# First two expert weight chunks split inside the eighth linear attention tile, a fourth split buffer for the first expert, gather rows cleared in that tile

## What is computed

```python
h = h + concat(o_gla, o_diff) @ w_out
xn = rms_norm(h, norm2_g)
g_w, g_idx = top_k(softmax(xn @ wg + bg), 1)        # one of 4 groups
e_w, e_idx = top_k(softmax(chosen group's 8 logits), 2)
for each of the 32 experts e, over the tokens routed to it:
    out[token] += weight * ((silu(x @ w1[e]) * (x @ w3[e])) @ w2[e])
```

## Time and profile before

| what | value |
|---|---|
| three runs | 1260.25, 1263.06 and 1264.33 us, median 1263.06 us |
| profiled execution | 1262.13 us |
| its span, first to last instruction | 1260.3 us |
| PE busy | 1162.5 us, 92% |
| DVE busy | 890.6 us, 71% |
| ACT busy | 690.3 us, 55% |
| POOL busy | 252.4 us, 20% |
| mean granted TensorE clock | 0.962 of full |

### The profile page before, as it was taken

The page is one execution under the profiler, slowest core; times in us unless marked ns, Lnnn a source line. Parts: engine busy times, 40 slices in busy tenths (PEclk is TensorE's granted clock), DMA queues, the critical chain, the costliest instruction groups (busy, mean ns, idle before and its releaser), DMA issues. The chain is left out here.

```text
span 1260.3 us, 17095 instructions
## 1 busy us (share of the span) xinstructions
PE 1162.5 (92%) x5875; PEld 875.0 (69%) x5876; DVE 890.6 (71%) x1310; ACT 690.3 (55%) x913; POOL 252.4 (20%) x324
## 2 busy tenths in 40 slices
PE   5989999889988779999669999999999999999993
PEld 4868887567766468888546777777777777777772
DVE  4434324655566467887658999999999999999881
ACT  5424204343543353343237777777777777777771
POOL 2212103321110021222341221221122122112100
PEclk9999999999999789999779999999999999999997
DMA  8030210200200243433479999999999999999941
GB/s 309 37 98 1 100 67 1 76 25 27 92 26 17 76 144 109 149 130 144 184 287 378 372 386 371 372 390 379 370 379 388 373 370 395 381 365 379 388 113 26
DMA packets 67426, 273.34 MB, mean 217 GB/s; under 512 B 13156, under 2 KB 19880, under 8 KB 42664
## 3 DMA queue, kind: packets, MB, share of 16 engines
q1 hardware_dynamic: 56744, 245.32, 50.5%
q0 software_dynamic: 7168, 20.98, 7.3%
q10 hardware_dynamic: 3456, 6.29, 1.3%
HBM read 248.44 MB, written 28.32 MB: 220 GB/s over the span
## 5 line engine op out<-in xcount | busy, mean ns | idle before, releaser
L1851 DVE TENSOR_TENSOR main_w_low<-w_raw,main_w_high 128x2048 fp32r<-128x2048 f32 x192 | 438.9, 2287 | 55.7 <-ACT main_w_high L1847 55.7
L1847 ACT CAST main_w_high<-w_raw 128x2048 fp32r<-128x2048 f32 x192 | 365.9, 1908 | 80.4 <-PE main_score L1865 52.6
L1777 POOL DMA_INDIRECT main_xg<-xn_dram,main_token x32 | 76.2, 2381 | 381.3 <-DVE main_token L1757 376.6
L1863 PE MATMUL main_pt<-main_w_high,main_xT_high 128*96 128x512 f32 x256 | 104.3, 408 | 1.2 <-DVE main_xT_low L2007 1.2
L1863 PE MATMUL main_score<-main_w_high,main_hT_high 128*96 128x512 f32 x256 | 103.2, 403 | 1.2 <-DVE main_hT_low L2019 1.2
L1863 PE MATMUL main_po<-main_w_high,main_xT_high 128*96 128x512 f32 x256 | 101.4, 396 | 2.8 <-DVE main_w_low L1851 2.8
L1865 PE MATMUL main_pt<-main_w_high,main_xT_low 128*96 128x512 f32 x256 | 102.8, 402 | 0.0
L1864 PE MATMUL main_pt<-main_w_low,main_xT_high 128*96 128x512 f32 x256 | 102.1, 399 | 0.0
L1865 PE MATMUL main_po<-main_w_high,main_xT_low 128*96 128x512 f32 x256 | 101.7, 397 | 0.0
L1865 PE MATMUL main_score<-main_w_high,main_hT_low 128*96 128x512 f32 x256 | 101.2, 395 | 0.0
L1864 PE MATMUL main_po<-main_w_low,main_xT_high 128*96 128x512 f32 x256 | 101.0, 395 | 0.0
(11 more groups left out here) (301 smaller groups left out, 2346.0 us busy)
## 6 DMA issues: line engine op xcount, KB each, us to landing
w_raw<-in_moe_w SPq DMA_DIRECT2D x192, 1024.0 KB, 10.4
slot_raw<-in_w_in SPq DMA_DIRECT2D x12, 1024.0 KB, 7.3
main_x<-in_x SPq DMA_DIRECT2D x8, 512.0 KB, 11.1
slot_raw<-in_w_out SPq DMA_DIRECT2D x4, 1024.0 KB, 6.3
main_hx<-in_x SPq DMA_DIRECT2D x8, 512.0 KB, 3.9
out<-main_hx SPq DMA_DIRECT2D x8, 512.0 KB, 2.6
xn_dram<-main_xn SPq DMA_DIRECT2D x8, 512.0 KB, 2.8
gr_dram<-main_stage ACTq DMA_DIRECT2D x8, 256.0 KB, 2.0
```

The lines of the kernel that those rows point to most:

```text
L1777: nc.gpsimd.indirect_dma_start(xg[u][:], None, s["xn2_dram"], bass.IndirectOffsetOnAxis(token[u][:, 0:1], 0), bounds_check=bound["x"], oob ...
L1847: nc.scalar.copy(wh[slot(c, e)][:], raw[u][c // 2][:, c % 2, :]).then_inc(w_high, 1)
L1851: nc.vector.tensor_tensor(wl[slot(c, e)][:], raw[u][c // 2][:, c % 2, :], wh[slot(c, e)][:].bitcast(F32), ALU.subtract).then_inc(w_low, 1)
L1863: nc.tensor.matmul(out, x_hi, w_hi, start=start, stop=False)
```

## The change

Six edits. (1) ACT casts chunks 0 and 1 of expert 0 at the end of its tile n = 7. (2) DVE subtracts chunk 0 in its tile n = 7, between `position` and `h_norm`; chunk 1 stays behind `list_token` but now waits until POOL's counter stands at the second gather. (3) DVE no longer makes the carried state after the last tile, which nothing reads; what waited for it waits for `g_o_mm`, PE's last product of that tile. (4) A fourth pair, `w_high3` and `w_low3`, takes chunk 5 of expert 0, so that the casts of its chunks 4 and 5 wait for the residual adds of tile 7 instead of a freed pair, and stand ahead of `act_x`; the raw buffer of these two chunks moves from 152 to 68 KiB. The first casts of expert 1 may run one chunk further ahead, and two loads of expert 2 wait for `chunk_used` 4. (5) SP issues chunks 0 and 1 of expert 1 at the start of n = 8 and chunks 4 and 5 of expert 0 after the first residual add of tile 7. (6) POOL clears `xg0` and `xg1` inside its tile n = 7.

```diff
-RAW_PAIRS = ((200, 104, 152), (168, 120, 136))
+RAW_PAIRS = ((200, 104, 68), (168, 120, 136))
...
+    def first_high(act, c):
+
+        act.wait_ge(s["raw_in"][0][c], 16)
+        nc.scalar.copy(w_first[0][c][:], s["raw_pair"][0][0][:, c, :]).then_inc(w_split_high, 1)
+
+    def first_low(dve, c):
+
+        dve.wait_ge(w_split_high, c + 1)
+        dve.wait_ge(g_o_mm, T)
+        nc.vector.tensor_tensor(w_first[1][c][:], s["raw_pair"][0][0][:, c, :], w_first[0][c][:].bitcast(F32),
+                                ALU.subtract).then_inc(w_split_low, 1)
...
             elif n == T:
-                sp.wait_ge(state_ready, T + 1)
-                for e, c in ((0, 4), (0, 5), (1, 0), (1, 1)):
-                    load_chunk(sp, a, s, e, e, c)
+                sp.wait_ge(g_o_mm, T)
+                for c in (0, 1):
+                    load_chunk(sp, a, s, 1, 1, c)
+                sp.wait_ge(added, 2 * T - 1)
+                for c in (4, 5):
+                    load_chunk(sp, a, s, 0, 0, c)
...
                     store_hxT(n - 1, half)
+                if n == T - 1:
+                    for c in range(2):
+                        first_high(act, c)
...
             h_root(n - 1)
+            if n == T - 1:
+                pool.wait_ge(g_o_mm, T)
+                clear_rows(0)
             if n < T:
                 g_root(n)
                 if n >= 2:
                     weights_of(pool, n - 2)
+            if n == T - 1:
+                pool.wait_ge(g_normed, T)
+                clear_rows(1)
...
-                carry(n)
+                if n + 1 < T:
+                    carry(n)
                 if n >= 2:
                     position(n - 2)
+                if n == T - 1:
+                    first_low(dve, 0)
...
         if isinstance(e, int) and e == 0:
-            return {0: 1, 1: 2, 4: 0, 5: 2}[c]
+            return {0: 1, 1: 2, 4: 0, 5: 3}[c]
...
         if isinstance(e, int) and e == 0:
-            if c == 5:
-                act.wait_ge(chunk_used, 2)
+            if c == 4:
+                act.wait_ge(after["added"], 2 * T - 1)
+            elif c == 5:
+                act.wait_ge(after["added"], 2 * T)
         else:
-            act.wait_ge(chunk_used, n - 1 if isinstance(e, int) and (e, c) == (1, 1) else n - 2)
+            act.wait_ge(chunk_used, n - 3 if isinstance(e, int) and e == 1 and c < 3 else n - 2)
...
             for k in range(2):
                 list_row(dve, k)
                 pick(q, k + 2, k + 2, k)
+                if k == 0:
+                    low(dve, 0, 0, 5)
...
     def scalar(act):
-        for chunk in range(2):
+        for chunk in (4, 5):
             high(act, 0, 0, 0, chunk)
         act_x(act, 0, 0)
...
-        for chunk in range(2):
-            low(dve, 0, 0, chunk)
+        dve.wait_ge(after["pool_step"], front["own"]["gathers"] + 2)
+        front["first_low"](dve, 1)
         dve_x(dve, 0, 0)
```

## The result

| kernel | median of its runs | ratio to before, 95% interval |
|---|---|---|
| before | 1262.88 us (1260.25 to 1264.33, 4 runs) | |
| after | 1253.96 us (1253.29 to 1255.11, 4 runs) | 0.9929 (0.9915 to 0.9943) |

A forecast was written before the change was run, and what follows sets the result against it. PE was taken to set the pace from expert 1 on, so an earlier expert start ends the kernel earlier. +3.8 - 4.6 - 7.2 = -8.0 us gave a forecast of 1254.7 us, range 1252.0 to 1260.3.

The forecast's parts named there:

- Term 1, the delay of `turn`: Tile 8: DVE's subtraction waits for ACT's cast and delays what follows; 3.2 us reach the chain through PE's `turn`.
- Term 1, the clock: Tile 8's output product on PE: after a longer gap it runs longer at the low clock, taken as 0.6 us.
- Term 2: First gather of expert 0: starting ahead of DVE's subtraction, it runs as if alone; -4.6 us, bounds -2.0 and -4.6.
- Term 3: Start of the experts, first gate chunk to expert 1's down product: PE's waits shrink; -7.2 us, bounds -5.7 and -8.1.
- two named parts: Expert 0 into expert 1: hidden transposes 5.7 us earlier, and the gate chunk behind them back at full clock, 1.5 us.
- the lower end: Lower end of the range, 1252.0 us: includes up to 0.6 less where the clock rises earlier in gate chunk 0.
- The cover of ACT's new casts: Casts of chunks 4 and 5 ahead of `act_x`: done at 631, transposes at 636.3, a cover of 5 us.
- The edits costed at nothing: POOL's clears and ACT's casts in tile 8, expert 1's later first loads, SP's wait for `chunk_used` 4: no cost.
- The caught gather: Rival at the first gather: one subtraction still catches it, gain only -2.0, sum -5.4, 1257.3 us; chance 0.30.
- The eaten head start: Rival: clock and new gaps, as at the hidden transposes, eat the gain; -3.4 to -1, 1259 to 1262 us; chance 0.16.
- The transfers: Rival from expert 1 on: transfers set the pace, SP's later loads make the kernel slower, 1263.9 us or more; chance 0.06.

The follow-up runs named there:

- three-pair kernel: The changed kernel with chunk 5 of expert 0 back in pair 2, its casts, expert 1's casts and SP's rule as before: 1260.10 us, ratio 0.9987.
- the counter alone: The kernel before with one edit, DVE's two subtractions behind the token lists wait for POOL's counter: 1256.35 us, ratio 0.9954.
- the three placements: Changed kernel, chunk 0's subtraction behind the counter, ahead of the last tile's first residual add, or between tile 8's sum and norm: 1250.27, 1249.84, 1249.91 us.

## Why the prediction was right

The forecast was 1254.7 us and the time 1253.96; the sum was -8.0, the medians differ by 8.9, and the profiled pair by 9.6 at the down product. That the total is so close owes something to luck: runs of the kernel before alone spread over 4 us, and two steps were off by 1.0 and 0.7 us. What speaks for the mechanism is the agreement step by step, from the anchor:

- **Term 1, the delay of `turn`: forecast +3.2, measured +3.25** (9.15 to 12.40), for the reason given: DVE sits idle 2.47 us for ACT's cast, then subtracts 2.29 us.
- **Term 1, the clock: forecast +0.6, measured -0.4.** This is the step that failed, and in sign. From `turn` to the first gather it is 22.76 us before and 22.35 after. I expected a longer low stretch in the output product. But the clock fell within the longer gap, at 609, and was up again near 615.8; the transposes of `turn` lost 0.5 us (1.12 instead of 0.64), the output product itself took 7.03 us against 7.17, and the router's product then ran at the full clock, 1.98 us instead of 2.74. I had priced the fall and not asked what would be running when the clock came back or fell next. The whole term is +2.8, just below its bounds of +3.2 to +4.3, and undoing it gave 2.9 to 3.6 at the down product (3.7 to 4.1 by the medians).
- **Term 2: forecast -4.6, measured -4.57** (from the gather's start to the transposes, 8.79 to 4.22), by itself on the kernel before -4.57 too. That it fits to the digit is chance: the gather took 1.26 us and not the 0.96 that I used, and the transposes came 2.96 us behind its end instead of 3.23. The narrow margin was rightly seen: with DVE 0.10 us behind, the gather goes on; with DVE 0.07 us ahead, it is caught (the kernel without the wait), and then half of the term is lost. The Trainium skill (SBUF — State Buffer, section SBUF: two separate sides) has the first to start hold the port for its whole instruction, while the other stands still. The gather, first, kept going as it says; but the subtraction, second, showed no wait (2.29 us, as alone).
- **Term 3: forecast -7.2, measured -7.9** (first gate chunk to down product, 31.84 to 23.98). Its two named parts came out as worked out: third gate chunk to hidden transposes -5.72 (forecast -5.7), hidden transposes to down product -1.54 (forecast -1.5). The remaining -0.6 lies ahead of the third gate chunk, where PE's clock rose near 643.1 instead of 645.5, the amount that I had put only into the lower end. The three-pair kernel shows that 1.4 of the 5.72 was no work of the pair but a fall of the clock in the profiled execution of before; I had taken it as part of the start times without seeing it, so that the profiled pair fits -5.7 is in this respect luck. The pair and its rule are worth 5.8 to 6.1.
- **The cover of ACT's new casts: forecast 5 us, measured 6.7.** The second cast ends at 630.01, the transposes start at 636.69.
- **The edits costed at nothing** cost nothing, shown for the carry and the clears together. That SP's new order of loads costs nothing is only read from the missing waits of ACT, and was not tried by itself; it may have its part in the lead that the transfers lost.
- **The rivals.** The caught gather is real and kept away by 0.1 us. The eaten head start did not come: the gap ahead of the hidden transposes is 0.58 us and the clock stays up. The transfers were not the bound, and less far from it than I wrote: I argued from a missing wait that they had room, and the lead turned out to be 12 us that nothing refills.

The parts add up: the counter alone gives 6 to 7, the pair 6, and the subtraction in tile 8 takes back 3 to 4: -8 to -10 for the whole, where -8.9 was measured. The better kernel keeps both gains and moves that subtraction: the three placements at 1250.3, 1249.8 and 1249.9 us are about 13 us faster than before (ratios of 0.989 to 0.990) and 4 faster than after, and cannot be told from each other.

## What to carry to other kernels

Where work is moved into idle time, ask which wait it lands in, not only whether the engine is idle somewhere near: one subtraction cost 3.3 us ahead of an operation that the chain needs and nothing two operations later, in the wait for another engine. When DVE and a gather on POOL start together, a wait that puts the gather first by a tenth of a microsecond can be worth the whole length of DVE's operation. And a transfer stream that no one waits for may still be exactly as fast as the compute: look at how the landing times move (medians of 10.4, 18.5 and 29.1 us here), since compute that speeds up behind the release of the stream, or a later release, eats a lead that is hardly refilled. A speed-up that moves the release as well does not.

## What the runs showed of the hardware

- **The clock's moment is not tied to the work.** The same wait of 2.77 us on PE was followed by 3 us at 0.50 in one kernel and by none in two others; the same 16 matmuls of the router took 1.98, 2.71 to 2.80, or 3.63 us. A term of 1 us that rests on one profile's clock is a guess.
- **POOL beside DVE.** A small POOL operation that began 0.23 us ahead of a subtraction ran as if alone, and so did the subtraction. Of gathers, one that began 0.10 us ahead ran 1.26 us and one that began 0.07 us behind ran 3.36. The margin is finer than the records tell: after the change a small cast on POOL at 640.30, recorded 0.05 us ahead of a subtraction at 640.35, took 2.47 us instead of 0.29. After the change, a gather of a later expert met DVE's closed row of operations and took 8.11 us, until DVE paused, without anyone waiting for it:

```profile
653.68 8.11 POOL L1814 DMA_INDIRECT main_xg<-xn_dram,main_token  x1 [1.26 <-issue]
```

- **The first gather costs 1.26 us and not 0.96**, with DVE idle as well (1.27). The second takes 0.96 to 0.97 alone, and 1.66 with a subtraction around its start.
- **Transfers at a share of 1.0 moved 378 GB/s before and 381 after from 700 to 1200 us, which was just this kernel's need.** A delay of 9 us at the start was still there 30 experts later.
